# Transposing the normed rows by DMA, with scale and shift applied in SBUF, in a two-layer hybrid decoder kernel

## What is computed

```python
def hybrid_layer(x, c, ...):
    h = adaln(rms_norm(x, g_mix), sh1, sc1)          # "mixing norm"
    proj = h @ w_in                                   # q, k, v of two attentions, two gates
    ...                                               # windowed attention, block-sparse attention
    mixed = sigmoid(gate_a) * y_a + sigmoid(gate_b) * y_b
    x = x + gt1 * (mixed @ w_out)
    h = adaln(rms_norm(x, g_mlp), sh2, sc2)           # "MLP norm"
    x = x + gt2 * (square(relu(h @ w_up)) @ w_down)
```

## Time and profile before

| | |
|---|---|
| time, median of 3 runs | 2123.86 us (2123.09 to 2240.29) |
| the profiled execution's own time | 2123.41 us |
| its span (slowest core, core 2) | 2121.9 us; the eight cores 2115.3 to 2121.9 us |
| granted TensorE clock, mean | 0.983 |
| busy: PE, DVE, ACT, POOL | 2003.4 us (94%), 1286.5 us (61%), 958.2 us (45%), 244.2 us (12%) |

### The profile page before, as it was taken

How to read it: one execution, slowest core, us unless ns; L and a number is a source line. 1 busy time by engine, 2 the same in 40 slices (tenths; PEclk the granted TensorE clock), 3 DMA queues, 4 the chain that set the end, 5 groups by cost and what they waited for, 6 DMA issues and landing times.

```text
span 2121.9 us, 36341 instructions; the slowest of 8 cores (2115.3 to 2121.9 us)
## 1 busy us (share of the span) xinstructions
PE 2003.4 (94%) x13004; PEld 942.1 (44%) x13004; DVE 1286.5 (61%) x2411; ACT 958.2 (45%) x1448; POOL 244.2 (12%) x246
## 2 busy tenths in 40 slices
PE   1899899999899999999999998999999999999999
PEld 1454344444454444444445443444444544444444
DVE  3689856463266566655569896564525665565665
ACT  2777664747645211111138776556685431111111
POOL 1336300000011000000002361000001010000000
PEclk9999899999999999999999997999999999999999
DMA  9967511010279181717330545101015905050022
GB/s 194 215 77 96 75 27 41 2 41 2 61 135 122 22 109 21 96 14 100 100 119 2 70 60 80 41 1 41 2 41 76 173 1 80 1 79 1 1 80 80
DMA packets 114926, 136.80 MB, mean 64 GB/s; under 512 B 3776, under 2 KB 100160, under 8 KB 113216
## 3 DMA queue, kind: packets, MB, share of 16 engines
q0 software_dynamic: 101200, 85.11, 29.4%
q1 hardware_dynamic: 13552, 49.37, 6.9%
HBM read 200.69 MB, written 18.87 MB: 103 GB/s over the span
## 4 chain that ended last, share of the span: by engine, by line
PE 90%; ACT 3%; issue 2%; DMA 2%; DVE 2%; SPq 0%; DVEq 0%; ACTq 0%
PE PS L625 88%; PE PS L635 2%; ACT SB L653 2%; DMA SB<-x 2%; DVE SB L658 1%; DMA SB<-w_ada 1%; DVE SB L684 0%; SPq L715 0%; ACT SB L886 0%; DVE SB L898 0%; DVE SB L694 0%; ACT SB L908 0%; ACT L653 0%; ACT SB L692 0%; DVE SB L674 0%
## 5 line engine op out<-in xcount | busy, mean ns | idle before, releaser
L625 PE MATMUL PS<-SB 128*128 128x512 bf16 (+4 forms) x12220 | 1971.7, 326 | 68.4 <-DMA SB<-w_ada 27.7
L625 PEld LDWEIGHTS PS<-SB 128*128 128x128 bf16 (+1 forms) x12220 | 890.6, 98 | 1090.4 <-issue 286.9
L653 ACT ACTIVATE SB<-PS 128x512 bf16<-128x512 f32 (+4 forms) x870 | 620.0, 737 | 922.0 <-PE PS L625 890.2
L658 DVE TENSOR_TENSOR SB<-SB 128x512 f32<-128x512 f32 (+7 forms) x711 | 456.7, 649 | 145.3 <-ACT SB L653 103.7
L658 DVE TENSOR_TENSOR SB<-PS,SB 128x512 f32<-128x512 f32 (+5 forms) x657 | 361.0, 557 | 136.0 <-PE PS L625 119.4
L684 DVE SCALAR_TENSOR_TENSOR SB<-PS,SB 128x512 bf16<-128x512 f32 x360 | 252.6, 705 | 265.1 <-ACT SB L653 264.7
L684 DVE SCALAR_TENSOR_TENSOR SB<-SB,PS 128x512 f32<-128x512 f32 x128 | 87.8, 686 | 160.9 <-PE PS L625 145.5
L658 POOL TENSOR_TENSOR SB<-SB 128x512 bf16<-128x512 f32 (+1 forms) x87 | 115.2, 1333 | 348.5 <-DVE SB L684 265.5
L635 PE MATMUL PS<-SB 128*128 128x128 bf16 x784 | 87.5, 229 | 45.5 <-DVE SB L898 23.8
L715 POOL DMA_DIRECT2D SB<-w_ada x48 | 40.0, 843 | 722.5 <-PE PS L625 691.9
L635 PEld LDWEIGHTS PS<-SB 128*128 128x128 bf16 x784 | 60.2, 102 | 84.3 <-issue 60.4
(11 more groups left out here) (25 smaller groups left out, 189.5 us busy)
## 6 DMA issues: line engine op xcount, KB each, us to landing
SB<-w_ada POOLq DMA_DIRECT2D x48, 512.0 KB, 9.2
SB<-w_in POOLq DMA_DIRECT2D x16, 1024.0 KB, 15.7
SB<-w_up POOLq DMA_DIRECT2D x16, 1024.0 KB, 11.4
SB<-w_down POOLq DMA_DIRECT2D x16, 1024.0 KB, 22.1
SB<-x SPq DMA_DIRECT2D x16, 512.0 KB, 13.6
SB<-x SPq DMA_DIRECT2D x8, 1024.0 KB, 7.8
xsp<-SB SPq DMA_DIRECT2D x4, 2048.0 KB, 7.5
SB<-xsp SPq DMA_DIRECT2D x8, 1024.0 KB, 7.1
```

What stands on the lines that cost most here:

```text
L625: ins = e.matmul(o.ap, l_.ap, rr.ap, start=a, stop=b)
L653: S.add([('act', lambda e, o=out, i=in_: e.activation(out=o.ap, in_=i.ap, func=func, **kw), d)], r, out.keys, tab=TABS.get(func))
L658: return e.tensor_tensor(out=o.ap, in0=a.ap, in1=b.ap, op=op)
```

## The change

All MLP norms and the mixing norms of layer 1 (12 of 16) no longer use PE. A DMA started by SP (`turn`) transposes each `xnb[tq]`, 128 x 1024 bf16 or 256 KB, straight into `dest[:, :, tq*128:(tq+1)*128]`; four for a norm, 48 in all. Then eight instructions apply scale and shift in place, SBUF to SBUF, bf16; each reads all 512 rows of its `kb` and so needs all four DMAs. They may now go to ACT, DVE or POOL, with an assumed DVE time at `fast` = 4. The four mixing norms of layer 0 stay as they were. `DVE_TAX` is zero and changes nothing.

```diff
+        def turn(out, in_):
+            dmac['sp'] += 1
+            S.add([('sp', lambda e, o=out.ap, i=in_.ap: e.dma_start(out=o, in_=i, transpose=True), 0.45)],
+                  in_.keys, out.keys, dma_key='sp%d' % (dmac['sp'] % 28), nbytes=512 * 1024)
@@ def norm
-        def norm(s, acol, bcol, dest):
+        def norm(s, acol, bcol, dest, by_dma):
...
+            if by_dma:
+                for tq in range(4):
+                    turn(dest[:, :, tq * 128:(tq + 1) * 128], xnb[tq])
             for kb in range(8):
-                pt = ps((512,), BF16)
-                for tq in range(4):
+                pt = dest[:, kb] if by_dma else ps((512,), BF16)
+                for tq in range(0 if by_dma else 4):
                     tr(pt[:, tq * 128:(tq + 1) * 128], xnb[tq][:, kb * 128:(kb + 1) * 128], identb)
...
-                S.add([('act', f_id, cost('act', 512) + 0.09), ('dve', f_ts, cost('dve', 512))],
-                      list(pt.keys) + list(a.keys) + list(b.keys), o.keys)
+                alts = [('act', f_id, cost('act', 512) + 0.09), ('dve', f_ts, cost('dve', 512, False, 4 if by_dma else 1))]
+                if by_dma:
+                    alts.append(('pool', f_ts, cost('pool', 512)))
+                S.add(alts, list(pt.keys) + list(a.keys) + list(b.keys), o.keys)
@@ kv_stage, MLP
-            norm(s, A1(l), modv(l)[:, 0:8], hTs(s))
+            norm(s, A1(l), modv(l)[:, 0:8], hTs(s), l > 0)
-                norm(s, A2(l), modv(l)[:, 24:32], h2(s))
+                norm(s, A2(l), modv(l)[:, 24:32], h2(s), True)
```

More of the change, by code:

```diff
@@ L26 @@
 FORM_COST = 0.095
+DVE_TAX = 0.0
 ENGS = ['pe', 'act', 'dve', 'pool', 'sp']
@@ L143, in release @@
                 for a in op['alts']:
-                    c = max(ready_t[i], free[a[0]] + backlog[a[0]]) + a[2]
+                    c = max(ready_t[i], free[a[0]] + backlog[a[0]]) + a[2] + (DVE_TAX if a[0] == 'dve' else 0.0)
                     if best is None or c < best[0]:
```

## The result

| | before | after |
|---|---|---|
| time, median | 2123.86 us | 2151.89 us (2145.0 to 2276.71, 5 runs) |
| ratio, 95% interval | | 1.0128 [1.0115, 1.014] |
| span of the slowest core in the profile | 2121.9 us | 2150.4 us |
| median span of the cores of die 0, die 1 | 2118.9, 2118.6 us | 2140.4, 2140.5 us |

The kernel became slower by 28 us, 1.3%, where I had forecast 6.5 us faster. (The highest run of each set is a disturbed one; the ratio leaves those out.)

A forecast was written before the change was run, and what follows sets the result against it. PE was taken as the bound nearly all the time from 580 us on, except at the layer border and the DVE-bound end of the query stage. -19.4 + 9.5 + 1.4 + 2 = -6.5 us gave 2117 us, range 2106 to 2166.

The forecast's parts named there:

- PE, 352 transposes: Transposes in full-clock matmul streams leave PE, 0.055 us each: -19.4 us.
- border, 0.7 + 4D: Between the layers, the first slice's four DMAs start after the spill and delay the first matmul: +9.5 us.
- D: Time from one 256 KB transposing DMA to the next, run one behind the other: taken as 2.2 us.
- clock after the border: After the longer idle stretch between the layers, PE's first matmuls run at half clock: +1.4 us.
- DMA sharing at the MLP norms: At slice 1 of the MLP norms, DMA engines already full with weights: 1 us in each layer, +2.
- rival 4: Query stage of layer 1: DVE is full, so PE's 5.3 us gain is lost; 2122 us, within the forecast's range.
- upper bound: Highest price of one transposing DMA, in pieces of 256 bytes at 83 ns, 64 per engine: 5.3 us.
- allowance: Time each norm's four DMAs have before DVE reaches the scale: MLP slices 12, 13, about 18 us; mixing 9.
- Rival 1: All transposing DMAs run at the spill's rate, about 0.64 to 1.5 us each: 2110 us, chance 0.17.
- Rival 2: DMAs slow, DVE's order passes the wait to PE: slower, up to 2207 us; chance 0.38, 0.16 above +2%.
- 32D - 94: Change in us when each DMA takes above 3.25 us, summed over border, mixing and MLP norms; 3.4 gives 2138.
- likeliest case: Each transposing DMA takes 1.5 to 2.8 us: 2112 to 2128 us for the whole kernel, chance 0.43.

The follow-up runs named there:

- big_copy: Changed kernel with each of the 48 transposing DMAs replaced by a plain, untransposed copy in 128 pieces of 2048 bytes: 2120.95 us, ratio 0.9986.
- mlp_01: Kernel before with only the MLP norms of slices 0 and 1 transposed by DMA, all others on PE: 2116.42 us, ratio 0.997.
- junk_mlp: Changed kernel with mixing norms back on PE and the squares' throw-away output sent to the norm's own destination: 2143.85 us, ratio 1.0091.

## Why the prediction was wrong

By its steps, measured by the sums of the stretches (2118.4 to 2141.0, +22.6):

| step | predicted | measured |
|---|---|---|
| PE, 352 transposes | -19.4 | about -16: big_copy is 14.1 shorter outside border and attention, with the clock's 2.2 in it; mlp_01 gave 7.0 for 7.0 |
| border, 0.7 + 4D | +9.5 | +7.1 |
| clock after the border | +1.4 | +2.2 |
| DMA sharing at the MLP norms | +2 | **+24.9** (big_copy against after: 12.4 + 12.5) |
| end of the attention (rival 4) | part of the range | +6.0 |
| sum | -6.5 | about +24 of +22.6 |

**What failed is the term "I add 1 us in each layer, +2".** No row showed that 1 us. I had looked at the DMA share where the norm of slice 1 stood, seen it full, and then priced the sharing at 1 us; slices 2 and 3 I passed over with "have more work in between, about 18 us". It was slice 2 that met the loads of `w_up` and `w_down`, and there D was 7.0 us and not 2.2. D was a constant in my sum, though it is a price that depends on who else is on the DMA engines. The working for the upper bound already held the tools: 64 pieces for each engine, 98.6 ns for a packet of weights. One weight packet after each piece gives 64 x (0.021 + 0.099) = 7.7 us, close to what was measured, and above the 5.3 that I had called the upper bound. I had bounded the duration of a piece, and not its waiting. (At that bound the prediction adds 9 us for slices 2 and 3; by its own allowance of 18 us it is 4 x 3.2 = 13.)

**D alone: better than taken.** 1.37 us for 2.2. Rival 1's price was right and its conclusion (2110 us) wrong. The 261 GB/s that the Trainium skill gives (*DMA: Bandwidth & Descriptors*, section "Latency and other measured facts") would be 1.0 us, and its 1309 ns for a block (*VectorE: DVE Perf Modes*, section "The three transpose paths") gives 10.5, both estimates; the trace lies at 191 GB/s, nearer the first. The rule of the second page (the Trainium skill, *VectorE: DVE Perf Modes*, section "Rules for kernel authors"), to use TensorE for a 128 x 128 transpose where PSUM will do, comes out right here for the norms beside weight loads (+24.9 us) and at the border (+7.1), but for another reason than the duration of a block.

**Border: right in size, wrong in what the DMAs wait for.** PE's gap was 15.4 us, near the 18 forecast. The first packet came 8.1 us after PE's last matmul, and the spill's end had been forecast for 8.6; that these agree is luck. The DMAs did not wait for the spill, which ended 1.6 us after their first packet, but for the last of the four rescales: they are issued 6.6 us after PE's last matmul, so without the spill little would be won. Then the four took 5.9 us instead of 8.8, and 1.4 us passed to the first matmul.

**The clock.** It is 0.58 over the 8 us behind the restart, so half clock for some 6 of them: 3.0 us lost, less the 0.8 of before. Keys and values took 3.3 us less, where -5.3 (96 x 0.055) + 2.2 gives 3.1.

**Rival 2, the slow DMAs, was nearest in outcome** (slower), but its sum 32D - 94 has the same fault: one D for all norms. And it looked at DVE alone. The longest wait in the kernel after was ACT's, for `xnb`, which the squares use as a bin (60.4 us for 20.8 on DVE); junk_mlp shows that without it DVE's wait stops PE as long (12.2 us in the first group, for 3.7 + 2.3 + 5.6). The allowance of a norm was not only the time to its scale instructions but also that to the next norm's squares.

**The scale instructions** cost 40.3 us on DVE in all, for 38 forecast, and DVE "no fuller than it was" held for keys and values (84% busy after, 86% before, on core 5). The range, 2106 to 2166, holds 2151.89; the likeliest case's own range does not, and the 2% were not reached, as the largest chance said.

## What to carry to other kernels

Price a DMA by its pieces and by its neighbours: pieces for each DMA engine times (own time + one packet of every other queue that is busy then), taken at each place where it will run, not once. As an estimate this gives 7.7 us for 7.0 measured with pieces of 256 bytes; with pieces of 2048 bytes it is low, 32 x (0.087 + 0.099) = 6.0 us for the 7.5 of slice 2 in big_copy. Then look for who waits for the source buffer to be read, not only for the destination. A change that moves a planner's order has a term of its own, here 12.5 us in 2120 without any change to the work. Read it first from the planner's total and its planned stretches, and replan the old kernel once to see how far they carry, before a gain of 6 us is believed. Keep an edit where its DMAs run alone or PE has enough work ahead of them (here slices 0 and 1 of the MLP, 0.997).

## What the runs showed of the hardware

- A transposing DMA of 256 KB in SBUF, 1024 pieces of 256 bytes, costs 1.37 us in a row with others when alone, and 7.0 us beside one queue of weight loads (packets of 512 and 1024 bytes, 90 to 93 ns each on average there). The ordinary copy in the same pieces gives the same time of the kernel within 3 us (2149.05 for 2151.89).
- 128 pieces of 2048 bytes instead: slice 2's four through in 7.5 us instead of 27.9, beside the same loads.
- To start one transposing DMA SP takes 1.28 us (median), for 0.69 for the plain copy in the same pieces and 0.50 for the one in large pieces.
- DVE's in-place scale, 128 x 512 bf16 with two per-partition operands, runs at 2.67 us for eight, 0.33 us each, when nothing else is going on.
